# Two-norm transitions of a two-block transformer kernel: normed rows of the first half issued among the second half's products, fewer weight slabs rounded meanwhile, row sums of four parts

## The reference, cut to what matters

```python
x = x + rms_norm(merged @ w_o, g_post_mix)      # norm 1, residual
hf = rms_norm(x, g_pre_ffn)                     # norm 2
f_gate, f_up = jnp.split(hf @ w_ffn_in, 2, axis=-1)
f = (jax.nn.silu(f_gate) * f_up) @ w_ffn_out
return x + rms_norm(f, g_post_ffn)              # norm 1, residual
...
h = rmsnorm(x, norm_w) * (1.0 + scale) + shift  # norm 2, second block
proj = h @ w_in

def rms_norm(x, g):
    y = x * lax.rsqrt(jnp.mean(x * x, axis=-1, keepdims=True) + EPS)
    return y * g
```

## Time and profile before

| | before |
|---|---|
| median of 3 runs | 2539.91 us |
| the runs | 2537.23, 2539.91, 6109.01 us |
| profiled execution | 2538.34 us |
| its span, first to last instruction | 2536.5 us |
| PE busy | 98% |
| POOL, DVE, ACT busy | 45%, 46%, 42% |
| mean granted PE clock | 0.995 of full speed |

### The profile page before, as it was taken

The page is one execution under the profiler, slowest core; times in us unless marked ns, Lnnn a source line. Parts: engine busy times, 40 slices in busy tenths (PEclk is TensorE's granted clock), DMA queues, the critical chain, the costliest instruction groups (busy, mean ns, idle before and its releaser), DMA issues.

```text
span 2536.5 us, 33040 instructions
## 1 busy us (share of the span) xinstructions
PE 2492.7 (98%) x13246; PEld 2144.4 (85%) x13246; DVE 1159.5 (46%) x2376; ACT 1060.3 (42%) x2026; POOL 1152.9 (45%) x682
## 2 busy tenths in 40 slices
PE   8999999999999999999999999999999999999998
PEld 7788888888888888888888888888898888898887
DVE  7672477756415782104234455522243335444313
ACT  4472498952325332224433433333344333333322
POOL 4354354554446355445444345444444444444442
PEclk9999999999999999999999999999999999999999
DMA  5233210135433453322222222222322222222232
GB/s 201 67 100 108 68 42 34 34 117 195 154 110 123 154 192 132 100 92 84 99 84 83 84 80 88 87 89 92 111 94 85 79 81 83 92 80 88 92 100 75
DMA packets 71769, 250.47 MB, mean 99 GB/s; under 512 B 7872, under 2 KB 12736, under 8 KB 71232
## 3 DMA queue, kind: packets, MB, share of 16 engines
q1 hardware_dynamic: 71616, 248.35, 28.8%
HBM read 246.22 MB, written 2.10 MB: 98 GB/s over the span
## 4 chain that ended last, share of the span: by engine, by line
PE 87%; DVE 6%; ACT 5%; POOL 1%; issue 1%; DMA 0%; SPq 0%; DVEq 0%; ACTq 0%; POOLq 0%
PE bank L1738 85%; PE bank L1748 2%; ACT PP L1956 1%; POOL w_lo L2804 1%; ACT pt_hi L1956 1%; ACT QQ L1956 1%; ACT w_hi L1956 1%; DVE pt_lo L2258 0%; DVE nt L2258 0%; DVE Y L2258 0%; DVE XR L2258 0%; DVE C L2258 0%; DVE PP L2511 0%; DMA XR<-in_x 0%; ACT Hhi L1956 0%
## 5 line engine op out<-in xcount | busy, mean ns | idle before, releaser
L2804 POOL TENSOR_TENSOR w_lo<-w_raw,w_hi 128x1024 fp32r<-128x1024 f32 (+1 forms) x319 | 760.6, 2388 | 878.2 <-ACT w_hi L1956 877.8
L1738 PE MATMUL bank<-Hhi,w_hi 128*128 128x512 f32 (+1 forms) x1676 | 653.8, 390 | 4.6 <-DVE XC L2266 4.6
L1738 PE MATMUL bank<-Hhi,w_lo 128*128 128x512 f32 (+1 forms) x1676 | 647.4, 386 | 0.0
L1738 PE MATMUL bank<-Hlo,w_hi 128*128 128x512 f32 (+1 forms) x1676 | 647.3, 386 | 0.0
L1956 ACT ACTIVATE w_hi<-w_raw 128x1024 fp32r<-128x1024 f32 (+1 forms) x319 | 325.9, 1026 | 121.0 <-DMA w_raw<-in_wa 81.7
L1738 PEld LDWEIGHTS bank<-Hhi,w_lo 128*128 128x128 f32 x1676 | 315.6, 188 | 65.1
L1738 PEld LDWEIGHTS bank<-Hhi,w_hi 128*128 128x128 f32 x1676 | 316.1, 189 | 62.6 <-DVE XC L2266 5.0
L1738 PEld LDWEIGHTS bank<-Hlo,w_hi 128*128 128x128 f32 x1676 | 316.3, 189 | 57.9
L2804 POOL TENSOR_TENSOR w_fifth_lo<-w_fifth_raw,w_fifth_hi 128x1024 fp32r<-128x1024 f32 (+1 forms) x79 | 192.3, 2435 | 227.2 <-ACT w_fifth_hi L1956 227.2
L1738 PE MATMUL bank<-Hhi,w_fifth_hi 128*128 128x512 f32 x404 | 161.2, 399 | 0.0
L1738 PE MATMUL bank<-Hhi,w_fifth_lo 128*128 128x512 f32 x404 | 157.7, 390 | 0.0
(11 more groups left out here) (413 smaller groups left out, 4876.3 us busy)
## 6 DMA issues: line engine op xcount, KB each, us to landing
w_raw<-in_wb SPq DMA_DIRECT2D x169, 512.0 KB, 3.4
w_raw<-in_wa SPq DMA_DIRECT2D x139, 512.0 KB, 3.3
wm<-in_w_ada SPq DMA_DIRECT2D x48, 512.0 KB, 4.4
w_fifth_raw<-in_wb SPq DMA_DIRECT2D x42, 512.0 KB, 3.4
w_fifth_raw<-in_wa SPq DMA_DIRECT2D x35, 512.0 KB, 3.3
wa_raw<-in_wb SPq DMA_DIRECT2D x5, 512.0 KB, 5.4
XR<-in_x SPq DMA_DIRECT2D x4, 512.0 KB, 7.7
w1k<-in_w1k SPq DMA_DIRECT2D x1, 2048.0 KB, 13.2
```

The costliest lines, as they stand in the source:

```text
L1738: return self.e.matmul(o, lhs, rhs, start=start, stop=stop)
L2804: self.e.tensor_tensor(x.lo[:, k:k + n, :], x.raw[:, k:k + n, :], f(x.hi[:, k:k + n, :]), ALU.subtract).then_inc(*w_rest(s, k))
```

## The change

It has five parts.

1. `normed` no longer sleeps 8 ticks after k = 1 but one tick after every second k (`pace=1`), so that rows k = 2 to 7 of half 0 are issued while half 1 of `first_parts` still runs.
2. `halves` rounds a slab only after the slab counts in `cuts`: after the second in the first transition (before: second to fifth), after the second and third in the second (before: second to fifth), after the second in the third (before: second to fourth). The slabs left out are rounded later, at the start of half 1 of `next_parts` and in the products behind.
3. `onto` works on two rows k at once: 4 multiplications and 4 additions of 128x2x256 on DVE instead of 8 and 8 of 128x256.
4. `N2.direct = 5`: rows 5, 6 and 7 go to PE as parts of their own, so that the row sums of norm 2 have four parts instead of two, and POOL adds four squares instead of six.
5. The counts of ticks in `two_norms` differ.

```diff
-        def halves(self, parts, before=None, after=None, deep=1, early=2):
+        def halves(self, parts, before=None, after=None, deep=1, cuts=()):
...
-                                if deep == 1 and over > early:
+                                if over in cuts:
                                     self.cut_to(self.cut, 4)
...
             for k in range(KT):
-                if k == 2 and gap:
-                    yield gap
+                if pace and k and k % 2 == 0:
+                    yield pace
...
-            for k in range(KT + 1):
-                if k < KT:
-                    self.o_times(name, dst, k, c, N1, [N1.m, o_ready[k, h]])
-                if k:
-                    self.x_add(name, dst, k - 1, c, before)
-                    x_ready[k - 1, h] = dve_o.by("x", name, k - 1, h)
-                    self.norm_add(N2, k - 1, XR[:, k - 1, c], x_ready[k - 1, h], c)
-            self.norm_read(N1, dve_o.by("times", name, KT - 1, h))
+            for k in range(0, KT, 2):
+                self.o_times(name, dst, k, c, N1, [N1.m, o_ready[k, h], o_ready[k + 1, h]])
+                self.x_add(name, dst, k, c, before)
+                for j in (k, k + 1):
+                    x_ready[j, h] = dve_o.by("x", name, k, h)
+                    self.norm_add(N2, j, XR[:, j, c], x_ready[j, h], c)
+            self.norm_read(N1, dve_o.by("times", name, KT - 2, h))
...
             c = HALF[h]
-            yield 2 if h else 1
-            yield from self.norm_end(N1, c, 3 if h else 1)
+            yield 1
+            yield from self.norm_end(N1, c, 2)
+            N2.direct = 5
             self.onto(c, name, dst, o_ready, N1, N2, x_ready, *before)
-            yield 9 if h else 12
-            yield from self.norm_end(N2, c, 1 if h else 3)
-            yield from self.normed(c, N2, lambda k, c: x_ready[k, c.start // 256], hs, scale, shift, H_free, *before, gap=8)
+            yield 9 if h else 11
+            yield from self.norm_end(N2, c, 2 if h else 3)
+            yield from self.normed(c, N2, lambda k, c: x_ready[k, c.start // 256], hs, scale, shift, H_free, *before, pace=1)
...
         def o_times(self, name, dst, k, c, N1, points):
             self.wait_ge(*points)
-            self.tt(dst[:, k, c], dst[:, k, c], N1.r, ALU.mult).then_inc(*dve_o("times", name, k, c.start // 256))
+            x = dst[:, k:k + 2, c]
+            self.tt(x, x, N1.r.unsqueeze(1).broadcast_to([128, 2, 256]), ALU.mult).then_inc(*dve_o("times", name, k, c.start // 256))
```

More of the change, by code:

```diff
@@ L629, in norm_read, with normed @@
             self.held.remove(N.b)
-        def normed(self, c, N, x_ready, hs, scale, shift, H_free, *before, by=None, gap=0, odds=(4, 6)):
+        def normed(self, c, N, x_ready, hs, scale, shift, H_free, *before, by=None, pace=0, odds=(4, 6)):
             gone = [None] * len(hs)
@@ L1090, in onto, with both @@
             h = c.start // 256
-            for k in range(KT + 1):
-                if k < KT:
-                    self.o_times(name, dst, k, c, N1, [N1.m, o_ready[k, h]])
-                if k:
-                    self.x_add(name, dst, k - 1, c, before)
-                    x_ready[k - 1, h] = dve_o.by("x", name, k - 1, h)
-                    self.norm_add(N2, k - 1, XR[:, k - 1, c], x_ready[k - 1, h], c)
-            self.norm_read(N1, dve_o.by("times", name, KT - 1, h))
+            for k in range(0, KT, 2):
[5 more added lines that the diff above has]
+            self.norm_read(N1, dve_o.by("times", name, KT - 2, h))
         def two_norms(self, h, name, dst, o_ready, N1, N2, x_ready, hs, scale, shift, H_free, *before):
             c = HALF[h]
-            yield 2 if h else 1
-            yield from self.norm_end(N1, c, 3 if h else 1)
+            yield 1
+            yield from self.norm_end(N1, c, 2)
+            N2.direct = 5
             self.onto(c, name, dst, o_ready, N1, N2, x_ready, *before)
-            yield 9 if h else 12
-            yield from self.norm_end(N2, c, 1 if h else 3)
-            yield from self.normed(c, N2, lambda k, c: x_ready[k, c.start // 256], hs, scale, shift, H_free, *before, gap=8)
-        def both(self, first_parts, next_parts, chain, name, *slots_free):
+            yield 9 if h else 11
+            yield from self.norm_end(N2, c, 2 if h else 3)
+            yield from self.normed(c, N2, lambda k, c: x_ready[k, c.start // 256], hs, scale, shift, H_free, *before, pace=1)
+        def both(self, first_parts, next_parts, chain, name, cuts, *slots_free):
             self.pump()
@@ L1117, in both @@
             H_free = self.H.spent
-            self.run(self.halves(first_parts, after=lambda h: tasks.append(self.later(chain(h, H_free))), early=1))
+            self.run(self.halves(first_parts, after=lambda h: tasks.append(self.later(chain(h, H_free))), cuts=cuts))
             self.run(self.halves(next_parts, before=lambda h: self.finish(tasks[h]), deep=4))
@@ L1449, in walk @@
                 lambda h, H_free: self.two_norms(h, "O", O, o_ready, n_post, n_pre, x_ready, hu[h], lambda k: P("g_pre_ffn", k), None, H_free, x_again),
-                "f", Y.spent)
+                "f", (2,), Y.spent)
             norm_done += [H.h[KT - 1][1], H.l[KT - 1][1]]
@@ L1545, in layer @@
                                for t, g in (("bk", 0), ("bk", 1), ("bk", 2), ("bq", 0))],
-                              x_chain, f"a{L}", *x_slots_free)
+                              x_chain, f"a{L}", (2,) if L else (2, 3), *x_slots_free)
             x_free = dict(x_ready)
@@ L2578, in x_add @@
             self.wait_ge(dve_o.by("times", name, k, h), *points)
-            self.tt(XR[:, k, c], XR[:, k, c], dst[:, k, c], ALU.add).then_inc(*dve_o("x", name, k, h))
+            x = XR[:, k:k + 2, c]
+            self.tt(x, x, dst[:, k:k + 2, c], ALU.add).then_inc(*dve_o("x", name, k, h))
         def first_gated(self, i):
```

## The result

The changed kernel is slower. Its median is 2549.81 us (2545.90 to 2553.14, six runs) against 2538.74 for the kernel before. The ratio is 1.0046, with a 95% interval of 1.0032 to 1.0059. That is 11 us more, where I had forecast 2540.4 us and a range up to 2545. One of the six executions of the kernel before took 6109.01 us; the ratio leaves it out, and without it that median is 2538.28 us, which makes the loss 11.5 us.

A forecast was written before the change was run, and what follows sets the result against it. PE, busy 98%, was taken as the bound. Gone 12.3 us; come row sums 3.2, square waits 2.8 + 4.7, clock 1.6 + 1.6, small waits 0.5, together 14.4: 2538.34 + 2.1 = 2540.4 us, range 2532 to 2545.

The forecast's parts named there:

- The bound, and the pricing of waits: PE, busy 98%, bounds the kernel; in both transitions a wait costs its idle time plus 0.16 us.
- My sign for a forecast wrong as a whole: PE's waits in the two transitions together fall below 5 us or exceed 12.
- The waits removed: First two transitions: PE's losses of 5.35 and 6.96 us, together 12.3, counted as gone.
- The last square: Norm 1, half 1: ACT's square behind eight Hhi rows makes PE wait 2.8 and 4.7 us in the two transitions.
- Rival C: The square isn't late and the change does all it can: 2529.2 us; chance 0.13.
- rows 2 to 7 "of half 0": Both transitions: half 0's rows come earlier, slabs later, so half 1's root waits behind no slab; slabs priced 0.
- The clock: Behind the square's new waits PE's clock falls to 0.50, costing 1.6 us in each of two transitions.
- Row sums of four parts: Norm 2, two halves, two transitions: 3.2 us more PE work, saving POOL two additions, 1.7 us.
- rival D: In onto, paired DVE additions stand back for POOL's: 2544.8 us; chance 0.17 together with slabs late behind the transitions.
- no term of the sum: Paired rows in onto: about 0.7 us shorter, contention uncertain, hidden by the products, so not counted.
- My 0: Third transition: no difference in time forecast, 0 us.
- My sum: Net loss over the transitions: +0.85 us in the first and +1.24 in the second, 2.1 together.

The follow-up runs named there:

- cuts alone: The kernel before with only the rounding of slabs changed, to the changed kernel's cuts: 2533.05 us, ratio 0.9978.
- Pairs alone: The kernel before with only paired rows in onto (two rows k at once): 2542.48 us, ratio 1.0018.

## Why the prediction was wrong

**The bound, and the pricing of waits.** Right. PE's waits and clock decide. Idle time plus 0.16 us makes the transitions add up to within about 1 us: from the rows of both kernels I get 2.8 us more for the first and 8.4 for the second, where 1.70 and 7.79 were measured. My sign for a forecast wrong as a whole, waits beyond 12 us in the two transitions, did not fire: they are 11.2 us (those of 0.15 and more), since the clock and the row sums, which took the rest, were no part of it.

**The waits removed.** Right for the slabs in the main. Without them in front of POOL's Hlo the first root was in time and the second 1.02 us late instead of 3.21, and cuts alone won 5.9 us. "I count the 12.3 us as gone" held in the changed kernel for the waits for the roots; POOL's last addition left 0.48 of 1.06.

**The last square.** The mechanism was right, the sizes 2.8 and 4.7 us against 2.54 and 3.56. The second was over-priced: I took the third transition's chain of 6.78 and added contention of 0.5, and there was none: the chain took 6.77 us (1179.74 to 1186.51). That is 1.1 us too much in all, which hid a part of the error below. Rival C, the square in time, is out with it.

**The step that failed: the rows of half 1.** I wrote that the change takes rows 2 to 7 "of half 0" earlier, and priced only these. The change sets the pace for both halves. In half 1 of the second transition the rows stand in front of the copies that free the banks of half 0's products, and PE waits for a bank twice more: 1.77 + 1.08 + 2 x 0.16 = 3.2 us, with 2.7 us of low clock around them, 5.9 in all, which my sum had at nothing. The kernel with the old placing in half 1 confirms the size: 5.2 us less in that transition, 6.4 by medians. For a step that is moved I should have asked in each half what it is moved past, and followed the banks as well as the H rows.

**The tick counts.** The change's fifth part had no term in my sum at all, and I gave no reason. In the changed kernel it brings the wait of 0.91 us for kB, 1.1 with the overlap; alone it cost 2.2 us in the two transitions.

**The clock.** Under-priced. I took 1.6 us for each transition because the wait of 3.21 us had cost that. The wait of 3.56 us cost 2.9, and the three short ones 2.7 together. In the first transition the forecast of 1.6 came out at 1.7, but not behind the wait that I had named: for 12 us behind the 2.54 the clock stayed at 1.00. That was this one execution. Three other kernels have the same wait (2.54, 2.54 and 2.53 us), and in all of them the clock fell within 2 us of it, for 1.7, 1.7 and 3.4 us lost. So the agreement of 1.6 and 1.7 is luck in the changed kernel's trace, and the rule behind it, a cost read off the length of the wait, was too simple. The kernel with two parts behind its 2.54 us:

```profile
814.00:816.00 2.00, 2.00 (x13) 2.00 (x13) 0.17 (x1) 0.26 (x1) 0.00 (x0) 0.65 0.00 0
816.00:818.00 2.00, 2.00 (x11) 2.00 (x11) 1.17 (x2) 0.00 (x0) 0.00 (x0) 0.50 0.00 0
```

**Row sums of four parts.** 0.9 us at each of four places (1.70 us from the first record to the next matmul, against 0.81), 3.6 where I had 3.2. My remark that they buy POOL 1.7 us in a chain where PE waited once was too weak beside pairs, where PE waits for POOL four times with two parts, since I took POOL's additions to stay at their length.

**Pairs, and rival D.** The step "no term of the sum" was wrong for the pairs by themselves: they cost 3.7 to 6.0 us. Rival D had the right mechanism with the roles exchanged. I expected DVE's additions to be held up, 1.2 us or more each, and they take 0.69; POOL's got longer instead, from 0.740 to 0.939 us with six and to 1.045 with four. The Trainium skill, page "SBUF — State Buffer", section "Who interferes with whom", says that the shared ports are an exclusive lock between the two engines. The traces agree in that additions with both inputs in SBUF got longer on either engine: beside pairs on POOL, and in the third transition on DVE, whose addition of nB (both inputs in SBUF, 128x256) lasts as long as a slab's rest on POOL beside it. The kernel before has the latter as well (2.42 us at 1839.45), so that it is no part of the loss. Timeline of the changed kernel, POOL and DVE:

```profile
1846.73 2.41 POOL L2807 TENSOR_TENSOR w_lo<-w_raw,w_hi 128x1024 fp32r<-128x1024 f32 x1 [1.04 <-ACT w_hi L1957]
...
1847.00 2.43 DVE L2259 TENSOR_TENSOR nB<-nB,nB 128x256 f32<-128x256 f32 x1 [2.78 <-ACT nB L1957]
```

An addition of that size takes 0.42 us with no company. In the changed kernel the four parts hid what the pairs do.

**Third transition.** My 0 was 0.95 short. Row sums wait 1.51 us instead of 0.55 for nB on DVE. On ACT of the changed kernel the rounding of a slab, which stands ahead of the square, waited for the slab to land, and before it did not, so that nB comes 0.98 us later behind the transition's first product than before (6.35 against 5.37 us):

```profile
1845.60 1.06 ACT L1957 ACTIVATE w_hi<-w_raw 128x1024 fp32r<-128x1024 f32 x1 [0.86 <-DMA w_raw<-in_wb]
1846.56 0.40 ACT L1957 ACTIVATE nB<-XR 128x256 f32<-128x256 f32 x1
```

This isn't due to the cuts: cuts alone took 49.47 us there. PE's longer wait for nB (1.44 to 1.85 us) occurred in all six kernels with four parts in both halves, and in none of the six others that have cuts, which took 49.46 to 49.48 us. On SP, too, the three issues of wa_raw that follow spread over 2.8 to 3.3 us in those six kernels and over 1.38 in all others. Why a few more matmuls 650 to 1000 us earlier should delay a transfer I can't say; I tried nothing that would tell, and it stays open.

What differs among the six is the clock. Three of them, the changed kernel among them, kept it and took 50.37 to 50.42 us; the others lost 1.7, 3.4 and 3.4 us to it and took 52.16, 53.34 and 53.61. Pairs alone shows how little the waits tell of it. It waited 0.56 and 0.24 us there, as the kernel before did (0.55 and 0.24), and yet its clock fell and the transition took 51.01 us:

```profile
1852.00:1854.00 2.00, 2.00 (x11) 2.00 (x11) 1.36 (x4) 0.91 (x2) 0.00 (x0) 0.50 0.00 0
```

**The whole.** My sum had 0.85 + 1.24 = 2.1; not forecast are 5.9 us for the half 1 rows, 1.1 for the tick counts, 1.3 for the clock behind the square, 1.0 for the third transition, 0.4 for row sums and 1.0 for small waits, less 1.1 for the square. That makes 2.1 + 9.6 = 11.7, where 10.4 was measured; the 1.3 between them are not explained.

## What to carry to other kernels

When a chain of side work is moved forward, list for every engine of it, and for each half or iteration that runs the same code, what now stands behind it: not only the values that PE reads but also the copies that give its banks back. Measure the parts of a bundled change one by one, since here one part was worth 6 us and the others together cost more than twice that. Leave the clock a range of its own: the same wait had a fall of the clock behind it in one execution and none in another. And where DVE and POOL add rows in SBUF at the same time, a longer instruction on one is a longer wait on the other; merging two instructions can lengthen the chain that was to be shortened.

## What the runs showed of the hardware

POOL's additions of 128x256 took 0.740 us on average beside DVE additions of 256 columns and 0.939 to 1.047 beside those of 512. DVE's took 0.592 on average beside POOL's in the first case, 0.42 without them; in the second they kept the 0.69 us that they take alone. Beside a slab's rest of 2.41 us DVE's addition of 0.42 took 2.43.

The granted clock didn't follow the waits. A wait of 2.54 us had a fall within 2 us of it in three kernels and none in a fourth. Cuts alone had 0.50 and 0.65 at 824 to 828 us behind a wait of 1.05, and the kernel before had 1.00 all through the same transition with waits of 2.05 and 1.06. With three or four parts in half 1 alone, where no wait of the first transition was above 0.32 us, no window fell in any of the three transitions, although the second had one of 1.02. Each kernel was profiled once, so that chance from one execution to the next can't be told from an effect of the program.

What a fall costs came in two sizes. Summed over its windows, the time lost if PE is busy throughout was 1.70 to 1.72 or 3.40 to 3.42 us in all 28 falls that the 14 traces have in the three transitions, the larger size behind the waits of 3.56 us and around the bank waits, among others.
